# The last expert tile finished by itself out of PSUM while the sums of all tokens are loaded, normed and stored

## What is computed

```python
def _hier_moe(x, rc_w, rc_b, rf_w, rf_b, w_gate, w_up, w_down):
    ...          # coarse top-1 group, then top-2 experts inside it; gates (t, 32)
    for e in range(MOE_EXPERTS):
        h = jax.nn.silu(t @ w_gate[e]) * (t @ w_up[e])
        out = out + gates[:, e:e + 1] * (h @ w_down[e])

x = x + _hier_moe(_rmsnorm(x, norm_ffn), ...)
y_prompt = _rmsnorm(xp, norm_final)[:, N_META:]
y_sample = _rmsnorm(xs, norm_final)
```

## Time and profile before

| | us |
|---|---|
| device time, median of 3 runs | 1093.66 |
| the 3 runs | 1087.75, 1093.66, 1093.88 |
| span of the profiled execution, first to last instruction | 1088.3 |
| PE busy in it | 980.5 |
| last matmul ends | 1065.3 |
| from there to the end | 23.0 |

### The profile page before, as it was taken

The page is one execution under the profiler, slowest core; times in us unless marked ns, Lnnn a source line. Parts: engine busy times, 40 slices in busy tenths (PEclk is TensorE's granted clock), DMA queues, the critical chain, the costliest instruction groups (busy, mean ns, idle before and its releaser), DMA issues.

```text
span 1088.3 us, 16989 instructions
## 1 busy us (share of the span) xinstructions
PE 980.5 (90%) x6432; PEld 691.6 (64%) x6433; DVE 450.8 (41%) x676; ACT 310.7 (29%) x597; POOL 332.4 (31%) x534
## 2 busy tenths in 40 slices
PE   6999999999999997999989999999878778988881
PEld 5889789786776786998765555555444434544440
DVE  6999876534456999862341111111101001111103
ACT  3025223542324352231332222222222121322123
POOL 1000888888303994000012222222221111221110
PEclk9999999999999898999999999999999899999996
DMA  7684171120099634346389999999999999999954
GB/s 261 123 143 83 38 128 60 39 62 20 18 276 210 197 110 164 117 195 268 131 316 399 394 385 403 388 395 406 403 391 402 392 415 411 415 414 415 422 225 164
DMA packets 73564, 277.54 MB, mean 255 GB/s; under 512 B 36952, under 2 KB 38872, under 8 KB 56496
## 3 DMA queue, kind: packets, MB, share of 16 engines
q1 hardware_dynamic: 63020, 252.67, 63.7%
q0 software_dynamic: 8720, 19.86, 6.7%
q10 hardware_dynamic: 1780, 4.41, 1.1%
HBM read 260.17 MB, written 25.61 MB: 263 GB/s over the span
## 4 chain that ended last, share of the span: by engine, by line
PE 65%; DMA 23%; DVE 8%; ACT 2%; issue 1%; SPq 0%; ACTq 0%; POOLq 0%; POOL 0%; DVEq 0%
PE ps L658 20%; DMA sb_arena<-w_up 20%; PE ps L1029 8%; PE ps L925 7%; PE ps L1043 7%; PE ps L1022 6%; DVE sb_y_lo L1736 2%; PE ps L998 2%; PE ps L777 2%; PE ps L690 1%; PE ps L803 1%; PE ps L746 1%; PE ps L828 1%; PE ps L824 1%; DMA x_scr<-sb_arena 1%
## 5 line engine op out<-in xcount | busy, mean ns | idle before, releaser
L658 PE MATMUL ps<-sb_arena 128*128 128x264 f32 (+1 forms) x1152 | 269.1, 395 | 9.8 <-DMA sb_arena<-wi 9.0
L658 PEld LDWEIGHTS ps<-sb_arena 128*128 128x128 f32 x1152 | 220.0, 192 | 58.9 <-DMA sb_arena<-wi 9.0
L1928 DVE TENSOR_TENSOR sb_s5b<-sb_s5b,ps 128x256 f32<-128x256 f32 x36 | 22.4, 621 | 415.2 <-PE ps L1029 415.2
L1029 PE MATMUL ps<-sb_arena 128*64 128x256 f32 x1152 | 139.6, 398 | 29.3 <-DMA sb_arena<-w_up 29.3
L1043 PE MATMUL ps<-sb_arena 128*64 128x512 f32 x576 | 131.6, 598 | 18.9 <-DVE sb_arena L1932 18.9
L1022 PE MATMUL ps<-sb_arena 128*64 128x256 f32 x1152 | 131.2, 380 | 11.4 <-DMA sb_arena<-w_gate 10.1
L1029 PEld LDWEIGHTS ps<-sb_arena 128*64 128x64 f32 x1152 | 86.8, 143 | 78.5 <-DMA sb_arena<-w_up 36.1
L1022 PEld LDWEIGHTS ps<-sb_arena 128*64 128x64 f32 x1152 | 83.4, 137 | 70.0 <-DMA sb_arena<-w_gate 21.7
L1376 ACT ACTIVATE sb_kxf<-ps,sb_gate_of 64x512 f32<-64x512 f32 x36 | 24.6, 682 | 314.7 <-PE ps L1043 314.7
L614 POOL COPY sb_idc<-sb_tok_of 64x1 int32 x36 | 6.4, 177 | 293.0 <-DMA sum_scr<-sb_kxf,sb_rwc 283.4
L1043 PEld LDWEIGHTS ps<-sb_arena 128*64 128x64 f32 x576 | 38.6, 136 | 88.6 <-issue 61.3
(11 more groups left out here) (309 smaller groups left out, 1264.4 us busy)
## 6 DMA issues: line engine op xcount, KB each, us to landing
sb_arena<-w_gate SPq DMA_DIRECT2D x32, 2048.0 KB, 34.1
sb_arena<-w_up SPq DMA_DIRECT2D x32, 2048.0 KB, 36.5
sb_arena<-w_down SPq DMA_DIRECT2D x32, 2048.0 KB, 36.4
sb_arena<-wi SPq DMA_DIRECT2D x28, 512.0 KB, 4.1
sb_arena<-w_out SPq DMA_DIRECT2D x4, 2048.0 KB, 8.6
sb_arena<-ssm_in POOLq DMA_DIRECT2D x8, 512.0 KB, 9.2
sb_arena<-wglu SPq DMA_DIRECT2D x8, 512.0 KB, 6.0
o_ssm_s<-sb_arena POOLq DMA_DIRECT2D x8, 512.0 KB, 3.9
```

The source lines that it names most:

```text
L658: last = mm(ps[:, b0 + h, 0:t1 - t0], ring[w % 3][:, k, :], src[:, k, t0:t1], start=k == 0, stop=k == KD - 1)
L1029: last = mm(ps[64 * r:64 * r + 64, 1, 0:256], xt[:, k, :], Wu[s][:, k, 256 * r:256 * r + 256], start=k == 0, stop=k == KD - 1)
L1928: V.tensor_tensor(hh.rearrange("p (j c) -> p c j", j=2), sg.rearrange("p (c j) -> p c j", j=2), ps[:, 1, 0:256].rearrange("p (c j) -> p c ...
```

## The change

The last tile (number `last_tile`, one less than the number of tiles) is taken out of the loops. ACT's loop is now one iteration per tile with computed addresses, where it was written out for four. It can no longer wait for a semaphore that depends on the buffer, so it waits for a new one, `rows_in >= q + 1`, that POOL counts up: once ahead of POOL's loop, and once in each of POOL's iterations, between the gather of tile j + 4 and the add of tile j, after a wait for the gather of tile j + 2.

POOL's adds take their tokens from `tok_add`, a copy of `tok_of` in which the last tile's column is absent rows, so that its 36th iteration moves nothing. SP loads the sums once the 35 adds of tiles 0 to 34 have landed. The last tile's down product stays in PSUM, in slot order, 128 rows of half a token (`2 * token + half`). POOL gathers the sums of its tokens as 128 half rows (`z_last`), DVE adds gate times PSUM, ACT and DVE norm it, and POOL scatters the half rows over `o_y` after all plain stores have landed. In the norm of the five parts, ACT's and DVE's steps for the last tile stand between those of parts 2 and 3 and of parts 3 and 4. Some semaphores are merged, with the same order.

```diff
+        xg_all = part(4288, RING * D, p=(0, T))
+        tok_add = part(4096, IDXC, p=(0, T)).bitcast(I32)
+        tok_last = part(4096 + IDXC, IDXC).bitcast(I32)
+        idx_last = part(4096 + 2 * IDXC, 1).bitcast(I32)
+        gate_last, ss_last, r_last = (part(4097 + 2 * IDXC + i, 1) for i in range(3))
+        z_last, sq_last, gfin_last = (part(512 * i, 512) for i in range(3))
...
@@ -516,7 +524,11 @@
             sp.dma_start(gfin, a["gfin"].partition_broadcast(P)).then_inc(moe_ld, 16)
-            sp.wait_ge(ye_ready, 1)
+            for r in range(2):
+                sp.dma_start(gfin_last[64 * r:64 * r + 64],
+                             a["gfin"][512 * r:512 * r + 512].partition_broadcast(64)).then_inc(moe_ld, 16)
+            last_tile = tile_bound(sp, slice(E + 1, E + 2), E - 1)
+            sp.wait_ge(yst, last_tile * 16)
             for i, (t0, n) in enumerate(TT):
                 sp.dma_start(G[i][0:n, 0], sum_scr[t0:t0 + n, :]).then_inc(gy[i], 16)
...
@@ -606,8 +619,16 @@
             pl.wait_ge(sum_st, 80)
             pl.wait_ge(gath[0], 16)
-            nt = tile_bound(pl, slice(E, E + 1), E)
-            with pl.Fori(0, (nt + RING - 1) // RING) as it:
+            pl.wait_ge(tab_ev, 3)
+            last_tile = tile_bound(pl, slice(E + 1, E + 2), E - 1)
+            nc.gpsimd.tensor_copy(tok_add, tok_of[:]).then_inc(pool, 1)
+            pl.wait_ge(pool, cnt[0] + 1)
+            nc.gpsimd.tensor_copy(tok_add[:, bass.ds(last_tile, 1)], tok_of[:, IDXC - 1:IDXC]).then_inc(pool, 1)
+            nc.gpsimd.tensor_copy(idx_last, tok_last[:, bass.ds(last_tile, 1)]).then_inc(pool, 1)
+            pl.wait_ge(pool, cnt[0] + 3)
+            pl.wait_ge(gath[1], 16)
+            pl.sem_inc(rows_in, 1)
+            with pl.Fori(0, (last_tile + RING - 1) // RING) as it:
...
+                    pl.wait_ge(gath[(u + 2) % RING], it * 16 + 16 + 16 * ((u + 2) // RING))
+                    pl.nop(nofuse=True)
+                    pl.sem_inc(rows_in, 1)
 
                     pl.wait_ge(yev, it * RING + u + 2)
...
+            halves = lambda v: v.rearrange("n (h d) -> (n h) d", h=2)
+            nc.gpsimd.indirect_dma_start(z_last, None, halves(sum_scr), bass.IndirectOffsetOnAxis(ap=idx_last, axis=0),
+                                         bounds_check=2 * N - 1, oob_is_err=False).then_inc(last_rows, 16)
             for u in range(RING):
-                pl.wait_ge(gath[u], ((nt + RING - 1) // RING) * 16 + 16)
+                pl.wait_ge(gath[u], ((last_tile + RING - 1) // RING) * 16 + 16)
             pl.nop(nofuse=True)
-            pl.sem_inc(ye_ready, 1)
+            pl.wait_ge(last_dve, 3)
+            pl.wait_ge(outs, 16 * 8)
+            nc.gpsimd.indirect_dma_start(halves(a["o_y"]), bass.IndirectOffsetOnAxis(ap=idx_last, axis=0), z_last, None,
+                                         bounds_check=2 * N - 1, oob_is_err=False).then_inc(last_rows, 16)
+            pl.wait_ge(last_rows, 32)
...
@@ -1361,31 +1388,51 @@
+            with ac.Fori(0, last_tile) as q:
+                ac.wait_ge(gmm, q + 1)
+                ac.wait_ge(hr, q + 1)
+                act_(sg, ps[:, 0, 0:256], ACT.Silu).then_inc(silu, 1)
+
+                ac.wait_ge(xtr, q + 2)
+                ac.wait_ge(rows_in, q + 1)
+                act_(xst, xg_all[:, bass.ds(((q + 1) % RING) * D, D)], ACT.Copy).then_inc(staged, 1)
...
+            ac.wait_ge(gmm, last_tile + 1)
+            ac.wait_ge(hr, last_tile + 1)
+            act_(sg, ps[:, 0, 0:256], ACT.Silu).then_inc(silu, 1)
+            ac.wait_ge(yo_free, last_tile + 2)
+            ac.sem_inc(staged, RING)
+            ac.sem_inc(yev, RING - 1)
...
+            for i in range(3):
+                token_square(i)
+                token_sqrt(i)
+            ac.wait_ge(last_dve, 1)
+            act_(sq_last, z_last, ACT.Square, accum_out=ss_last).then_inc(last_act, 1)
+            token_square(3)
+            ac.wait_ge(last_dve, 2)
+            act_(r_last, r_last, ACT.Sqrt).then_inc(last_act, 1)
+            token_sqrt(3)
+            token_square(4)
+            token_sqrt(4)
...
+            dv.wait_ge(moe_ld, 112)
+            for i in range(3):
+                token_root(i)
+            dv.wait_ge(dmm, last_tile + 2)
+            dv.wait_ge(last_rows, 16)
+            dv.wait_ge(last_act, 1)
+            V.scalar_tensor_tensor(z_last, ps[:, 4, :], gate_last, z_last, ALU.mult, ALU.add).then_inc(last_dve, 1)
+            dv.wait_ge(last_act, 2)
+            link(V.tensor_tensor(r_last[0:64], ss_last[0:64], ss_last[64:128], ALU.add))
+            link(V.tensor_tensor(r_last[64:128], ss_last[64:128], ss_last[0:64], ALU.add))
+            V.tensor_scalar(r_last, r_last, 1.0 / D, EPS, ALU.mult, ALU.add).then_inc(last_dve, 1)
+            token_root(3)
+            dv.wait_ge(last_act, 3)
+            link(V.reciprocal(r_last, r_last))
+            V.scalar_tensor_tensor(z_last, z_last, r_last, gfin_last, ALU.mult, ALU.mult).then_inc(last_dve, 1)
+            token_root(4)
```

More of the change, by code:

```diff
@@ L227, in build @@
             "p (a t) -> p a t", t=IDXC) for i in range(2))
-        yo = [kxf[0:T, D + 1024 * u:D + 1024 * u + 1024] for u in range(2)]
+        yo_all = kxf[0:T, D:3 * D]
+        yo = [yo_all[:, D * u:D * u + D] for u in range(2)]
         s5b = sb("s5b", [P, 14 * G5])
@@ L318, in build @@
             "idc_done", "staged", "xtr", "xev", "gmm", "umm", "silu", "hr", "htr", "hev", "dmm", "yev"))
-        rwc_done, yst, yo_free, ye_ready = sem("rwc_done"), sem("yst"), sem("yo_free"), sem("ye_ready")
+        rwc_done, yst, yo_free = sem("rwc_done"), sem("yst"), sem("yo_free")
         sum_st = sem("sum_st")
@@ L322, in build @@
         fo_done, wr_done = sem("fo_done"), sem("wr_done")
+        rows_in, last_rows, last_dve, last_act = (sem(x) for x in ("rows_in", "last_rows", "last_dve", "last_act"))
         gsrc = a["w_gate"].rearrange("e (p k) n -> e p k n", k=KD)
@@ L1363, in _ @@
             ac.sem_inc(staged, 1)
-            with ac.Fori(0, (nt + RING - 1) // RING) as it:
-                for u in range(RING):
-                    q = it * RING + u
-                    ac.wait_ge(gmm, q + 1)
-                    ac.wait_ge(hr, q + 1)
-                    act_(sg, ps[:, 0, 0:256], ACT.Silu).then_inc(silu, 1)
-                    ac.wait_ge(xtr, q + 2)
-                    ac.wait_ge(gath[(u + 1) % RING], it * 16 + 16 + 16 * ((u + 1) // RING))
-                    act_(xst, xg[(u + 1) % RING], ACT.Copy).then_inc(staged, 1)
-                    ac.wait_ge(dmm, q + 2)
-                    ac.wait_ge(yo_free, q + 1)
-                    act_(yo[u % 2][:, 0:512], ps[0:64, 4, :], ACT.Copy, scale=gate_of[0:64, bass.ds(q, 1)])
-                    act_(yo[u % 2][:, 512:1024], ps[64:128, 4, :], ACT.Copy,
-                         scale=gate_of[64:128, bass.ds(q, 1)]).then_inc(yev, 1)
-                ac.nop(nofuse=True)
@@ L1380, in _ @@
-            ac.nop(nofuse=True)
+            ac.wait_ge(tab_ev, 3)
+            act_(gate_last, gate_of[:, bass.ds(last_tile, 1)], ACT.Copy).then_inc(last_act, 1)
+            with ac.Fori(0, last_tile) as q:
[5 more added lines that the diff above has]
+                act_(xst, xg_all[:, bass.ds(((q + 1) % RING) * D, D)], ACT.Copy).then_inc(staged, 1)
+                ac.wait_ge(dmm, q + 2)
+                ac.wait_ge(yo_free, q + 1)
+                act_(yo_all[:, bass.ds((q % 2) * D, 512)], ps[0:64, 4, :], ACT.Copy, scale=gate_of[0:64, bass.ds(q, 1)])
+                act_(yo_all[:, bass.ds((q % 2) * D + 512, 512)], ps[64:128, 4, :], ACT.Copy,
+                     scale=gate_of[64:128, bass.ds(q, 1)]).then_inc(yev, 1)
+                ac.nop(nofuse=True)
@@ L1537, in _ @@
                     link(last)
-            last.then_inc(wp_done, 1)
+            last.then_inc(vt_done, 1)
             dv.wait_ge(ld_misc, 96)
@@ L1611, in _ @@
             dv.wait_ge(lc_mm, 16)
-            V.tensor_scalar(strict, tri, -1.0, 1.0, ALU.mult, ALU.add).then_inc(strict_set, 1)
+            V.tensor_scalar(strict, tri, -1.0, 1.0, ALU.mult, ALU.add).then_inc(de_in, 1)
             link(V.memset(dE, 0.0))
@@ L1882, in _ @@
             link(V.tensor_copy(cum[0:1, 0:E + 1], incl[0:1, :]))
+            ts(cum[0:1, E + 1:E + 2], incl[0:1, E:E + 1], -1.0, None, ALU.add)
             stt(rank, bc(incl[:, 0:E], 1, 5), float(T), ps[:, 7, 256:256 + 5 * E].rearrange("p (i e) -> p i e", i=5),
@@ L1918, in _ @@
             V.tensor_tensor(xt, ps[:, 2, :].rearrange("p (k t) -> p k t", k=KD), bc(g8, 2, T), ALU.mult).then_inc(xev, 1)
+            for r in range(2):
+                V.tensor_scalar(tok_last[64 * r:64 * r + 64], ps[0:T, 6, 256:256 + IDXC], -2.0, 2.0 * ABSENT + r,
+                                ALU.mult, ALU.add).then_inc(tab_ev, 1)
             dv.wait_ge(slot_done, 1)
-            nt = tile_bound(dv, slice(E, E + 1), E)
+            last_tile = tile_bound(dv, slice(E + 1, E + 2), E - 1)
@@ L1939, in token_root @@
+            turned(last_tile + 2, last_tile + 1)
```

(9 more changed lines are left out.)

62 lines of the change are left out of this document (32 added, 30 removed).

## The result

The changed kernel takes 1099.6 us (median of four runs, 1097.93 to 1100.83); the kernel before, run beside it, takes 1091.34 (four runs, 1087.75 to 1093.88). The ratio is 1.0093, with a 95% interval of 1.0075 to 1.011: slower by about 0.9%, some 8 to 10 us (8.3 between the medians; the interval reaches from 8.2 to 12.0). The profiled execution is the one of 1097.93 us; its span is 1096.1, so 1.8 us lie around it. The span before was 1088.3, so 7.8 us are to be found.

A forecast was written before the change was run, and what follows sets the result against it. DMA was taken as full, with PE's own pace to 767, the weight stream to 1056, then the tail. Span 1088.3 + 4.6 (start) - 1.3 (tail) = 1091.6; its 3.3 on the median 1093.66 gave 1097.0 us, range 1090 to 1103.

The forecast's parts named there:

- Only then may POOL scatter: 0.9 + 3.5.: End of the tail: after the last store lands, POOL's scatter takes 0.9 of preparation and 3.5 to land.
- The start of the loop: Tile 0: ACT's first copy waits for POOL's `rows_in`; 4.6 us of the lateness reach the weight stream (bounds 1.3 to 5.6).
- about 1056: End of the weight stream: the last up product starting there in spite of the late start would show the prediction wrong.
- Half clock: PE behind the wait at tile 0: a spell at half clock adds 1.7 us (0 to 3.4).
- The two engines hold each other near 11 us late: Loop after tile 0: PE and POOL both run about 11 us late (9.1 to 12).
- Hidden lateness: Weight stream near the gate load at 689.25: queued transfers hide 6.4 us of lateness (7.8 at the upper bound).
- The tail: From tile 34's add to the end: about 27 us against 28.3 before, ending at 1087.0, 1.3 us earlier.
- The small edits: In the loop: ACT's table load per tile, computed addresses, DVE's small steps and merged semaphores cost nothing.
- Rival 1: Tail: the absent add lands at once, at 1066.6; the end comes 1.4 earlier, 1095.6 us; chance 0.14.
- Rival 2: Weight stream: the start's lateness stays hidden and only the tail counts, 1092.4 us; chance 0.14.
- rival 3: Tail: POOL's absent add and gather pay full-queue prices, `z_last` later than 1073.7; 1104.8 us; chance 0.12.
- Rival 4: Tail: the sums' loads are held until the last tile, no overlap, tail longer by 4.4; 1102.7 us; chance 0.03.

The follow-up runs named there:

- the early signal: Kernel after, with the first `rows_in` given as soon as tile 1's rows have landed: 1095.12 us, 1.0045 of the kernel before.
- the held copy: Kernel before, with ACT's first copy of rows waiting for POOL's signal that tile 0's rows have landed: 1093.43 us, 1.0025 of the kernel before.
- the held copies: Kernel before, ACT's first copy held until tile 2's rows landed (1087.56 us), until tile 0's rows landed (1093.43), or that plus 40 memsets (1097.16).
- drain alone: Kernel after, with only GpSimd's closing drain left out: 1092.61 us, 1.0024 of the kernel before.
- both mended: Kernel after, with GpSimd's closing drain left out and the first `rows_in` given once tile 1's rows have landed: 1084.88 us, 0.9973 of the kernel before.
- POOL held to the end: Kernel before, with POOL waiting until all stores have landed, so its closing drain starts last: 1095.79 us, 1.0049 of the kernel before.
- parts first: Kernel after, without closing drain, first `rows_in` early, and all five parts normed before `z_last`: 1082.29 us, 0.9957 of the kernel before.

## Why the prediction was right in its range and not in its sum

Forecast were 1097.0 us in a range of 1090 to 1103, slower by 3.3 and within 1%. Measured were 1099.6 and slower by 8 to 10, still within 1% (the interval reaches 1.1%). The mechanisms of the two terms that I worked out held. A third term, larger than both, is missing from the sum: the range was wide enough to hold it, for no reason that I had given. Some of the closeness is luck too. The 3.3 were laid on a median of 1093.66, and the kernel before came out at 1091.34 with one run more, so 8.3 slower looks like 2.6 above the forecast.

**The missing term.** The step that failed is the end of the tail: "Only then may POOL scatter: 0.9 + 3.5." I took the landing of the scatter for the end of the program. I priced the scatter by what POOL needs ahead of a transfer and what the transfer needs to land, but not by what stands behind POOL's last instruction. The drain of 6644 ns stood in the trace of before, at 1072.1, under its norms. Three runs pin it down: leaving it out of the kernel after gives back 7.0, putting it at the end of the kernel before costs 5.7, and leaving it out there, where it is hidden, changes nothing (1087.43 against 1087.28).

**The start of the loop** was forecast at 4.6 and measured at 4.5 by the early signal and 3.3 by the held copy alone, each give or take 2 us or more, and at 2.0 to 3.1 by the traces. "The last weight some 4.6 later" did not show in the profile: the last up product came 1.2 later, 2.0 without the drift, close to the "about 1056" that I had named as a sign of being wrong. The early signal and the held copies show that the path is right; its size was put too high, by an amount that stays open. Within it:
- The first turn was forecast 9.1 late. From the turn before it, it stood at 18.36 instead of 10.91: 7.5. Most of the difference is the landing of tile 0's rows: POOL's load of its bound, which follows it, starts at 571.3 where it started at 573.6, 1.5 earlier once the drift of 0.75 is taken off (of these, 0.8 are that the gathers were issued earlier, 558.89 against 560.44). From there to PE's turn it took 3.1, and the forecast had 3.2.
- Half clock was forecast at 1.7 and found at 1.6 (5.25 against 3.65) in the product behind the wait; by the next turn, 1.9 had been added. In the forecast of POOL's first add I left it out, though the add waits for that product.
- That POOL paces itself and holds the later copies did not happen in the kernel after. Its index copies waited for its adds (593.90, behind 7.53 of idleness), but PE's turns kept 12.47 from tile to tile. So the lateness was 9.3 and not 11. "The two engines hold each other near 11 us late" rested on one iteration of 36, and the trace after doesn't bear it out. POOL does hold copies once the first signal is early: there PE ends up 4 to 5 late, and the stream hides it.
- Hidden lateness was forecast at 6.4 from one load's landing and found at 5.5 to 6 from the medians of three kernels and at 6.4 to 7.4 from the traces. 11 - 6.4 is 4.6, and 9.3 less what is hidden is 2 to 4. The lateness is what was clearly too high.
- The first wait for a weight came later than 767, as named: behind 1.71 of idleness at 809.17, where the kernel before waited 0.21 at 773.10 and 1.96 at 778.73. That the gate load near 700 lands in under 10 us can't be checked, as the trace of the kernel after has no landing for it.

**The tail** was forecast at 27.0 from the index copy behind tile 34's add to the scatter's landing, and took 27.1. Its steps were off in both directions, so the sum is better than its terms:

| step | forecast | measured |
|---|---|---|
| to the start of the absent add | 3.1 | 3.0 |
| its landing | 4.9 | 6.3 |
| to the landing of the gather | 4.4 | 5.4 |
| `z_last` to the end of part 4 | 7.65 | 7.2 |
| store of part 4 | 2.3 | 1.9 |
| scatter, with its preparation | 4.4 | 3.3 |

The absent add beside the loads of the sums took longer than forecast. So did the gather, but only in the two traces with the drain; where that is left out its step is 4.0 (drain alone) and 4.3 (both mended), against the forecast's 4.4. The scatter took less. With both mends the gain against the kernel before was 2.4 (0.12 to 0.41% by the interval, 1.3 to 4.5 us), and the forecast of 1.3 is its lower edge; why it is a little more wasn't tried by itself.

**The small edits** cost nothing that could be seen. The table load stands in each of 35 tiles at 1.28, and leaves 0.54 of idleness ahead of the SiLU while PE sets the pace, near the 0.68 in the earlier trace rows. PE's last turn waited 0.80 for ACT, forecast at some 0.7, with nobody behind it.

**The rivals.** Rival 1 is out: the absent add landed after 6.26 us, with the sums' loads under way. The Trainium skill ("DMA: Bandwidth & Descriptors", Queues, rings and completion order) has each DMA engine take turns between its queues packet by packet. What I drew from that, an empty transfer that waits for a packet or so, is not borne out by this row. The turns themselves may still be so, as no run shows what a transfer of absent rows does in these microseconds. Rival 2 (all lateness hidden) falls with the early signal, whose gain of 4.5 has an interval clear of zero, and with the held copies. Rivals 3 and 4 gave the differences nearest to the measured 8 to 10 (11.1 and 9.0), and neither happened. The gather's landing, 14.7 behind the index copy, is later than rival 3's turning point of 13.7, but the steps behind it gave that back. Rival 4 has the sums' loads held back, and they went out 2.2 ahead of the last down product.

## What to carry to other kernels

Look at what each engine's queue still has to do behind its last instruction, and ask of a moved step not only when it lands, but which engine is now last: an engine whose closing time is hidden costs it in full once it ends the program. A wait added early in a kernel that is later bound by a stream of loads costs its length less what is queued (here some 5.5 to 7.4 us); two or three kernels with the wait at different lengths test that reserve, where the landing of one load only suggests it. Where medians move by some us from series to series, compare the traces stretch by stretch as well. And a change that is slower as a whole can hold a gain: here two side effects of 7.0 and 4.5 us, by the medians, hid 2.4, and the change with them removed, and its last steps in a better order, is 5 us faster than the kernel before.

## What the runs showed of the hardware

- **GpSimd's closing drain took 6.6 to 6.8 us**, whether its last transfer was issued 2.6 us (1086.51 to 1089.1) or 20 us (1071.66 to 1091.9) ahead of it. In the kernel after, the last drain of SP took 0.01, of ACT 0.23 and of DVE 1.3 us.
- **TensorE's clock fell to half at this place in some executions and not in others**, and not in those with the longer wait ahead: the down product behind a wait of 1.61 us took 3.65 us before, with a granted clock of 1.00, which is 2.4 GHz, and 3.65 behind 1.47 (signal early) and 1.38 (POOL held to the end). It took 5.35 behind 1.22 (both mended), 1.07 (parts first) and 0.99 us, part of it at 1.2 GHz. The last is the kernel before with the drain left out, whose program is the same up to here. A stretch of the run with both mends (560 to 575, in steps of 5 us) shows it in the granted clock, the number ahead of the DMA share:

```profile
560.00:565.00 5.00, 3.78 (x36) 3.22 (x33) 0.60 (x1) 1.44 (x2) 1.56 (x2) 1.00 1.04 321
565.00:570.00 5.00, 4.48 (x19) 1.86 (x20) 1.02 (x2) 0.00 (x0) 0.00 (x0) 0.69 0.99 336
570.00:575.00 5.00, 5.00 (x40) 2.70 (x38) 0.00 (x0) 2.65 (x3) 1.91 (x7) 0.96 1.04 439
```

  So the product moved by 1.7 us with nothing in the program to account for it. Two of the three at full clock (signal early, POOL held) ran on one chip, and the three at half on another; whether the chip or the single execution decides stays open.
- **Transfers of absent rows alone are not free:** beside the loads of the sums one took 6.3 us from issue to landing, not much less than the full add ahead of it, beside the last weights (7.3). In quiet queues a gather of absent rows took 2.0.
